# Turning a decode cache's keys: 128x128 transposes on TensorE against 32x32 block turns on VectorE with block transfers, and a changed order of two quads

## The reference

```python
kw = jnp.concatenate([ck_win, k_win], axis=1)          # 512 cached window rows + 4 new
vw = jnp.concatenate([cv_win, v_win], axis=1)
kc = rope(compress(concat(gather_pages(ck_cmp), k_cmp)), cend)
o_cmp, o_sel, o_win = nsa_core(q, pos, kc, vc, cend, overlap, gather_sel, kw, vw, kpos)
```

## Time and profile before

| | |
|---|---|
| median of 3 runs | 589.26 us (589.05 to 589.99) |
| the profiled execution, its own time | 592.85 us |
| its span in the trace | 591.1 us |
| TensorE busy | 560.5 us (95%) |
| VectorE busy | 335.8 us (57%) |
| ScalarE busy | 266.2 us (45%) |
| GpSimd busy | 135.2 us (23%) |

### The profile page before, as it was taken

How to read it: one execution, slowest core, us unless ns; L and a number is a source line. 1 busy time by engine, 2 the same in 40 slices (tenths; PEclk the granted TensorE clock), 3 DMA queues, 4 the chain that set the end, 5 groups by cost and what they waited for, 6 DMA issues and landing times.

```text
span 591.1 us, 12729 instructions
## 1 busy us (share of the span) xinstructions
PE 560.5 (95%) x5102; PEld 505.4 (85%) x5102; DVE 335.8 (57%) x830; ACT 266.2 (45%) x601; POOL 135.2 (23%) x237
## 2 busy tenths in 40 slices
PE   6899999999988999998899999999999999999994
PEld 4899999989977899797689787676778999999994
DVE  5633222488748665336327548858766257773465
ACT  5434435444413352433233267767777253223333
POOL 0016323121101121460330005556453300000000
PEclk9899999999969999999999999999999999999998
DMA  9437722553227234492382215755355533415103
GB/s 300 167 93 220 255 73 71 213 175 128 78 68 243 82 92 123 144 333 95 96 296 72 69 41 142 192 149 143 92 151 134 149 110 108 144 37 176 42 8 145
DMA packets 59468, 80.51 MB, mean 136 GB/s; under 512 B 7249, under 2 KB 48145, under 8 KB 59154
## 3 DMA queue, kind: packets, MB, share of 16 engines
q1 hardware_dynamic: 48320, 49.44, 26.9%
q0 software_dynamic: 10368, 29.14, 15.8%
q10 hardware_dynamic: 722, 1.12, 0.5%
HBM read 65.23 MB, written 8.13 MB: 124 GB/s over the span
## 4 chain that ended last, share of the span: by engine, by line
PE 60%; DVE 5%; ACT 2%; issue 1%; ACTq 0%; DVEq 0%
PE m L1698 40%; PE s L2005 4%; PE o L2012 3%; PE t L1907 1%; PE s L1880 1%; PE s L1881 1%; PE s L1883 1%; PE o L1966 1%; PE t L1844 1%; PE s L1921 1%; PE m L1782 1%; PE o L1992 1%; PE t L1985 1%; DVE w_lo L1272 1%; PE t L1978 1%
## 5 line engine op out<-in xcount | busy, mean ns | idle before, releaser
L1698 PE MATMUL m<-h_hi,w_hi 128*128 128x272 f32 x448 | 134.0, 299 | 0.5 <-DVE w_lo L1272 0.5
L1698 PE MATMUL m<-h_hi,w_lo 128*128 128x272 f32 x448 | 129.2, 288 | 0.0
L1698 PE MATMUL m<-h_lo,w_hi 128*128 128x272 f32 x448 | 128.8, 287 | 0.0
L1698 PE MATMUL m<-w_hi,h_hi 128*128 128x256 f32 (+2 forms) x360 | 105.4, 293 | 2.8 <-issue 1.9
L1698 PE MATMUL m<-w_lo,h_hi 128*128 128x256 f32 (+2 forms) x360 | 102.8, 286 | 0.0
L1698 PE MATMUL m<-w_hi,h_lo 128*128 128x256 f32 (+2 forms) x360 | 102.8, 286 | 0.0
L1272 DVE TENSOR_TENSOR w_lo<-raw,w_hi 128x1024 fp32r<-128x1024 f32 (+2 forms) x62 | 71.1, 1154 | 42.9 <-ACT w_hi L1003 42.9
L1698 PEld LDWEIGHTS m<-h_hi,w_hi 128*128 128x128 f32 x448 | 84.2, 188 | 12.3 <-issue 10.9
L1698 PEld LDWEIGHTS m<-h_lo,w_hi 128*128 128x128 f32 x448 | 84.5, 189 | 0.0
L1698 PEld LDWEIGHTS m<-h_hi,w_lo 128*128 128x128 f32 x448 | 84.5, 189 | 0.0
L955 POOL DMA_DIRECT2D U<-p_turn x108 | 58.1, 546 | 102.7 <-DVE p_turn L1604 94.8
(11 more groups left out here) (296 smaller groups left out, 961.3 us busy)
## 6 DMA issues: line engine op xcount, KB each, us to landing
raw<-in_w_in SPq DMA_DIRECT2D x36, 512.0 KB, 3.8
U<-in_x_p SPq DMA_DIRECT2D x8, 512.0 KB, 5.4
raw<-in_w_o SPq DMA_DIRECT2D x8, 512.0 KB, 3.7
U<-p_turn POOLq DMA_DIRECT2D x54, 64.0 KB, 2.5
U<-p_turn SPq DMA_DIRECT2D x42, 64.0 KB, 2.9
raw<-in_w_in SPq DMA_DIRECT2D x8, 256.0 KB, 3.2
U<-in_ck_win POOLq DMA_DIRECT2D x8, 256.0 KB, 3.2
U<-in_cv_win POOLq DMA_DIRECT2D x8, 256.0 KB, 6.3
```

The source lines that it names most:

```text
L1698: ins = mm(out, lhs(a, k), rhs(b, k), start=(k == 0 and a + b == 0), stop=(k == n - 1 and a == 1))
```

## The change

The keys are no longer turned by TensorE. Step `kt` is now VectorE's alone: two 32x32-block transposes of 128x256 from the key ring into a buffer `key_turn` (two of them). A new step `km` moves the chunk's 16 blocks of 32 partitions x 512 floats (64 KB each) to their places in `keysT` (two buffers): ten from SyncE, six from GpSimd, each behind a wait for the chunk's four turns (`wait_keys_free`). `qkS` waits for the moves. The key ring has four slots, freed by VectorE's turns. GpSimd loads the selected values of the first quad between the turns of chunk 2 (`load_values`) and the others in a new step `v_load`. The order of the stretch is written out anew; it holds the same 19 `main` groups. Scores of the second quad's chunk 0 come ahead of the first quad's `s_exp`, those of chunk 1 after its `s_scale`, those of chunk 2 after its `s_out`.

```diff
@@ -152,10 +152,6 @@
-AFTER_KEYS = (1, 1, 1)
-AFTER_STEP = [(1, 1, 1, 1, 1, 1),
-              (1, 1, 1, 1, 1, 1)]
-
@@ -278,19 +274,48 @@
+
+    def keys(q, c):
+        order.extend(("kt", q, c, b) for b in range(QB))
+
+    keys(0, 0)
+    order += [("km", 0, 0)]
     main(1)
     order += [("mix", u1[3]), ("kc", NCH - 1)]
-    for q in range(NQ):
-        for c in range(3):
-            order += [("kt", q, c, b) for b in range(QB)]
-            main(AFTER_KEYS[c])
-            order += [("qkS", q, c)]
-        for n, step in enumerate(("s_max", "s_turn", "s_imp", "s_mask", "s_exp", "s_scale")):
-            if (q, step) == (NQ - 1, "s_scale"):
-                order += [("cs", 0)]
-            order += [(step, q)]
-            main(AFTER_STEP[q][n])
-        order += [("s_pv", q), ("s_out", q)]
+    main(1)
+    keys(0, 1)
+    order += [("km", 0, 1)]
+    main(1)
+    order += [("qkS", 0, 0)]
+    main(1)
+    keys(0, 2)
+    order += [("km", 0, 2)]
+    main(1)
+    order += [("qkS", 0, 1)]
+    main(2)
+    order += [("qkS", 0, 2), ("s_max", 0), ("v_load", 0)]
+    keys(1, 0)
+    order += [("km", 1, 0)]
+    main(1)
+    order += [("s_turn", 0)]
+    main(1)
+    order += [("s_imp", 0)]
+    keys(1, 1)
+    main(1)
+    order += [("s_mask", 0)]
+    main(1)
+    order += [("qkS", 1, 0), ("km", 1, 1), ("s_exp", 0)]
+    main(1)
+    keys(1, 2)
+    order += [("s_scale", 0)]
+    main(1)
+    order += [("qkS", 1, 1), ("km", 1, 2), ("s_pv", 0), ("s_out", 0), ("qkS", 1, 2), ("v_load", 1)]
+    for step in ("s_max", "s_turn", "s_imp", "s_mask", "s_exp", "s_scale"):
+        if step == "s_scale":
+            order += [("cs", 0)]
+        order += [(step, 1)]
+        main(1)
+    order += [("s_pv", 1), ("s_out", 1)]
@@ -411,8 +436,6 @@
-    if kind == "kt":
-        return ["act" if s[2] == 2 or (s[2] + s[3]) % 2 == 0 else "dve"]
@@ -429,9 +452,11 @@
-KEY_RING = 2 * RING
+KEY_RING = 4
...
+KEYS_AT = (0, 1, 0, 1, 1, 1)
+KEYS_BY_SYNC = 10
@@ -453,7 +478,7 @@
-    return load_turned(len(LOADS) - RING + n // 2) if n < KEY_RING else T_AT[KEYS[n - KEY_RING]] + 1
+    return load_turned(len(LOADS) - RING + n // 2)
@@ -560,7 +585,7 @@
-        key_ring = U[:, 8192:11264].rearrange("p (r c) -> p r c", r=KEY_RING)
+        key_ring = U[:, 8192:10240].rearrange("p (r c) -> p r c", r=KEY_RING)
@@ -574,8 +599,9 @@
-        keysT = U[:, 6144:8192].rearrange("p (b n) -> p b n", b=QB)
-        ptr = [U[:, 7680:8192], U[:, 12928:13440]]
+        keysT = [U[:, 4096:6144], U[:, 6144:8192]]
+        key_turn = [(prm[:, 0:1024], prm[:, 1024:2048]), (placed("key_turn", 3072, [P, 1024])[:, :], U[:, 10240:11264])]
+        ptr = [pm("b_sp"), U[:, 12928:13440]]
@@ -620,6 +646,8 @@
+        key_turned = sem("key_turned")
+        k_moved, k_moved_pool = [sem(f"k_moved{n}") for n in range(2)], [sem(f"k_moved_pool{n}") for n in range(2)]
@@ -668,15 +696,29 @@
+        def key_move(q, c, n):
+
+            f, a = divmod(n, 4)
+            src = key_turn[(3 * q + c) % 2][f // 2][32 * a:32 * a + 32, 512 * (f % 2):512 * (f % 2) + 512]
+            return keysT[KEYS_AT[3 * q + c]][32 * f:32 * f + 32, 512 * a:512 * a + 512], src
+
+        def wait_keys_moved(eng, q, c):
+
+            n = 3 * q + c
+            eng.wait_ge(k_moved[n % 2], 16 * KEYS_BY_SYNC * (n // 2 + 1))
+            eng.wait_ge(k_moved_pool[n % 2], 16 * (16 - KEYS_BY_SYNC) * (n // 2 + 1))
+
...
-            if 3 * q + c:
-                eng.wait_ge(qk_done, 3 * q + c)
+            n = 3 * q + c
+            eng.wait_ge(key_turned, QB * (n + 1))
+            if n == 0:
+                eng.wait_ge(hid_sum, NCH)
+                eng.wait_ge(out_done, 16 * N_OUT)
+            elif n == 1:
+                eng.wait_ge(kc_ready, NCH)
...
-                eng.wait_ge(out_done, 16 * N_OUT)
-                eng.wait_ge(kc_ready, NCH)
-            if q and c == 0:
-                eng.wait_ge(o_done, q)
+                eng.wait_ge(qk_done, max(m for m in range(n) if KEYS_AT[m] == KEYS_AT[n]) + 1)
@@ -806,6 +848,11 @@
+                elif s[0] == "km":
+                    _, q, c = s
+                    wait_keys_free(sp, q, c)
+                    for n in range(KEYS_BY_SYNC):
+                        sp.dma_start(*key_move(q, c, n)).then_inc(k_moved[(3 * q + c) % 2], 16)
@@ -895,7 +942,10 @@
-                pool.wait_ge(t_done, key_freed(n))
+                if n < KEY_RING:
+                    pool.wait_ge(t_done, key_freed(n))
+                else:
+                    pool.wait_ge(key_turned, n - KEY_RING + 1)
@@ -903,6 +953,11 @@
+
+            def load_values(b):
+                n = b % QB
+                pool.indirect_dma_start(U[:, n * 1024:n * 1024 + 1024], None, cv_sel,
+                                        bass.IndirectOffsetOnAxis(rows_sb[:, b:b + 1], 0)).then_inc(v_loaded, 16)
@@ -956,19 +1011,26 @@
-                    if c < 2:
-                        continue
-                    if n == 0:
-                        if q == 0:
+                    if (q, c) == (0, 2):
+                        if n == 0:
...
-                            pool.wait_ge(kc_done, NCH)
-                            pool.wait_ge(kc_ready, NCH)
-                        else:
-                            pool.wait_ge(o_done, q)
-                    b = QB * q + n
-                    pool.indirect_dma_start(U[:, n * 1024:n * 1024 + 1024], None, cv_sel,
-                                            bass.IndirectOffsetOnAxis(rows_sb[:, b:b + 1], 0)).then_inc(v_loaded, 16)
-                    pool.dma_start(U[:, 4096 + n * 512:4608 + n * 512], cv_win[b].rearrange("(m r) c -> m (r c)", r=4)).then_inc(v_loaded, 16)
+                        load_values(n)
+                elif s[0] == "km":
+                    _, q, c = s
+                    wait_keys_free(pool, q, c)
+                    for n in range(KEYS_BY_SYNC, 16):
+                        pool.dma_start(*key_move(q, c, n)).then_inc(k_moved_pool[(3 * q + c) % 2], 16)
+                elif s[0] == "v_load":
+                    q = s[1]
+                    if q == 0:
+                        pool.wait_ge(qk_done, 3)
+                    else:
+                        pool.wait_ge(o_done, 1)
+                        for n in range(QB):
+                            load_values(QB + n)
+                    for n in range(QB):
+                        pool.dma_start(U[:, 4096 + n * 512:4608 + n * 512], cv_win[QB * q + n].rearrange("(m r) c -> m (r c)", r=4))\
+                            .then_inc(v_loaded, 16)
@@ -1129,11 +1191,6 @@
-                elif kind == "kt" and t_uses(s) == ["act"]:
-                    _, q, c, b = s
-                    act.wait_ge(t_done, t + 1)
-                    wait_keys_free(act, q, c)
-                    nc.scalar.copy(keysT[:, b, :], TB[t % 2][:, :]).then_inc(t_act, 1)
@@ -1452,11 +1509,21 @@
-                elif kind == "kt" and t_uses(s) == ["dve"]:
+                elif kind == "kt":
...
-                    dve.wait_ge(t_done, t + 1)
-                    wait_keys_free(dve, q, c)
-                    v.tensor_copy(keysT[:, b, :], TB[t % 2][:, :]).then_inc(t_dve, 1)
+                    ld = KEY_AT[s]
+                    n = 3 * q + c
+                    dve.wait_ge(key_loaded[ld % KEY_RING], 16 * (ld // KEY_RING + 1))
+                    if b == 0:
+                        if n >= 2:
+                            wait_keys_moved(dve, *divmod(n - 2, 3))
+                        elif n == 1:
+                            dve.wait_ge(hid_sum, NCH)
+                    src = key_ring[:, ld % KEY_RING, :].rearrange("p (m h f i) -> p h m f i", m=4, h=2, f=2)
+                    for h in range(2):
+                        dst = key_turn[n % 2][h].rearrange("p (f b m i) -> p b m f i", f=2, b=QB, m=4)[:, b, :, :, :]
+                        ins = v.transpose(dst, src[:, h, :, :, :])
+                    ins.then_inc(key_turned, 1)
@@ -1900,25 +1967,22 @@
-                elif kind == "kt":
-                    ld = KEY_AT[s]
-                    pe.wait_ge(key_loaded[ld % KEY_RING], 16 * (ld // KEY_RING + 1))
-                    for m in range(4):
-                        ins = pe.transpose(tb[:, m * P:(m + 1) * P], key_ring[:, ld % KEY_RING, m * P:(m + 1) * P], ident)
-                    ins.then_inc(t_done, 1)
...
-                    for b in range(QB):
-                        wait_evacuated(pe, T_AT[("kt", q, c, b)])
+                    wait_keys_moved(pe, q, c)
...
-                    elif c == 0:
+                    elif q and c == 0:
+                        pe.wait_ge(s_bias2, q)
+                    elif q and c == 2:
...
+                    kx = keysT[KEYS_AT[3 * q + c]].rearrange("p (a b m i) -> p b a m i", a=4, b=QB, m=4)
...
-                        ins = mm(S[c][32 * b:32 * b + 32, :], q_bd[:, QB * q + b, :], keysT[:, b, :], start=True, stop=True)
+                        out = S[c][32 * b:32 * b + 32, :].rearrange("p (m a i) -> p a m i", m=4, a=4)
```

(1 more changed line is left out.)

## The result

The changed kernel takes 605.4 us (median of 4 runs, 600.95 to 607.75) against 589.25 on the same chip: 1.0263 times the time, 95% interval 1.0198 to 1.0327. It is slower, by 2.0 to 3.3%; I had forecast 588.5, and 592.6 as the upper end. The profiled execution took 606.87 us, its span is 605.1, 14.0 more than before.

What follows compares the result with a forecast made beforehand. TensorE, busy for 95% of the span, and its waits bound the kernel. Gone 17.7 us, come 17.6, plus 0.7 of fewer switches: 0.8 earlier, 589.26 - 0.8 = 588.5 us, range 585.2 to 592.6.

Steps and rivals of the forecast that it cites:

- 15.1 + 0.8 + 1.8 + 0.7: TensorE time gone: key transposes 15.1, a wait for weights 0.8, old clock fall 1.8, fewer transpose/group switches 0.7 us.
- ahead of (0,1): First quad, chunk 1: TensorE there at 249.6, keys moved at 251.4, a wait of 1.8 us.
- ahead of (0,2): First quad, chunk 2: TensorE there at 258.6, keys through full transfer engines at 265.3, a wait of 6.7 us.
- ahead of (1,0), `s_mask`: Second quad, chunk 0: scores wait for `s_mask`, whose banks they overwrite, until 283.1; a wait of 2.2 us.
- ahead of (1,1): Second quad, chunk 1: keys moved at 294.2, TensorE there at 290.4 after only two groups; a wait of 3.8 us.
- around the value products: Second quad, chunk 2: moves covered by the first quad's value products; start 303.9 against 295.2 + 7.2, 1.5 us.
- 8.4 us from turned to moved: Each chunk: SyncE's ten moves, the tenth starting after 9 x 0.65 = 5.85 us and landing 2.6 us later.
- the second rival: First quad, chunk 2: gathers hold back GpSimd's six moves, last landing 7.4 us after issue; 592.4 us, chance 0.18.
- one fall of the clock: After the 6.7 us wait of the first quad's chunk 2, TensorE's clock falls once to half, costing 1.6 us.
- the third rival: TensorE's clock falls at every wait, mostly hidden in later waits; 1.9 us more, 590.4 us, chance 0.15.
- VectorE matters only where it is named above: VectorE gains 17 us of turns and loses 8 copies; costed at nothing outside the walked-through steps.
- The two rivals on the slow side: Gathers holding back GpSimd's moves (592.4 us, chance 0.18) and the clock falling at every wait (590.4 us, chance 0.15).

Runs made afterwards that it cites:

- Run 1: Changed kernel with GpSimd's four gathers of the first quad's selected values issued behind its six moves of the third chunk; 599.49 us, one of four runs at 589.91.
- Runs 2: Changed kernel with matmuls of no use ahead of the waits for moved keys of the first five chunks; 603.62 us, 1.0241 times the kernel before.
- run 9: run 5's kernel with matmuls of no use ahead of the waits for keys of (0,0), (0,2), (1,0), (1,1); 594.28 us, 1.0054 times the kernel before.
- Run 3: Changed kernel without the 96 block moves, scores reading the turned blocks in place (wrong elements); 590.55 us, 1.0017 times the kernel before.
- run 6: Run 3's kernel (no moves, wrong elements) with VectorE's later turns as in run 5; 586.25 us, 0.9935 times the kernel before.
- runs 5: Run 1's kernel with VectorE's turns of (1,1) put behind `s_mask` and of (1,2) behind `s_scale`; 596.29 us, 1.0136 times the kernel before.
- run 8: run 7's kernel with both quads' value gathers issued later on GpSimd, not ahead of key gathers; 586.5 us, 0.9937 times the kernel before.
- run 7: Kernel before, TensorE's transposes issued in pairs one group ahead, third key buffer, (1,0)'s scores between `s_pv` and `s_out`; 598.97 us, 1.0168 times.

## Why the prediction was wrong

What went was put at 15.1 + 0.8 + 1.8 + 0.7 = 18.4, and the balance of the measured sum leaves 18.6: this part was right, as far as a balance can say. What came was put at 17.6 and measured 32.6. By its terms:

| term | forecast | measured |
|---|---|---|
| wait ahead of (0,0) | 0 | 2.0 |
| ahead of (0,1) | 1.8 | 0 |
| ahead of (0,2) | 6.7 | 12.8 |
| ahead of (1,0), `s_mask` | 2.2 | 2.9 |
| ahead of (1,1) | 3.8 | 0 |
| around the value products | 1.5 | 3.1 (`s_scale`) |
| half clock | 1.6 | 10.4 |
| other (a gap of 0.75, modelled ends 0.7) | 0 | 1.4 |

**The step that failed first: "8.4 us from turned to moved".** Its issue part was right (0.7 apart), its landing part was not. I took 2.6 us, from moves of the prompt's attention, where the queues together take 0.47 of the transfer engines' time (419 to 461 us). Here the last move landed 4.0 us after its issue at (0,0) and 7.5 at (0,2); from turned to moved it was 10.5 us at (0,0) (233.88 to 244.39). The rows that should have priced it stood beside it: the earlier trace rows with a share of 0.97 and the earlier trace rows, where a gather in the same stretch takes up to 7.4. I used the 7.4 for the second rival, with a chance of 0.18, and not for the sum; there the full engines moved the landing at (0,2) by 0.7 only, through 5.0 MB at 320 GB/s. Measured were 5.30 MB, and 262 to 264 GB/s. At (0,2) the keys came at 273.1, forecast 265.3: 3.3 us of the 7.8 are GpSimd's moves issued later (265.57 against 262.3, mostly because the turns ended 3.5 late, behind groups that the first wait had delayed), 4.5 are the landing. That GpSimd's six stand behind eight gathers was foreseen. Run 1 shows that the place of the four value gathers, on GpSimd's queue and on the transfer engines together, was worth 8.4 us of that wait.

**The second: one fall of the clock, "1.6".** I counted one and got four, 10.4 us, the largest term of the miss. It was the third rival, at 0.15, and I priced even that at 1.9, on the ground that a fall is hidden in the next wait. It is not, where the next wait ends with VectorE, which is late by the same amount. On this the Trainium skill, "TensorE: Matmul & The Clock Gate", section "HAM oscillation — how this bites in real kernels", was the better guide than my one row: by that rule the clock falls at each of the four waits, and the trace agrees, with 0.50 to 0.57 behind each. Runs 2 and 9 show that the clock can be bought back, but part of the time went into later waits (run 9: ahead of (1,1) from 1.0 to 2.7). So the 10.4 are not what would be gained without them, and what the clock alone costs stays open: in run 9's kernel 2 us by the medians, 5 by the ratios and 0.5 by the two profiled executions. Run 1's one execution at 589.91, with a clock of 0.987, may say that it is more; no trace of it is there.

**The third: "VectorE matters only where it is named above".** The turns are 16 us (six times 2.7) on an engine that works in order, and they put waits for transfers ahead of softmax steps. Run 3 takes all moves away and is no faster than before; run 6 takes the turns from ahead of two softmax steps as well and gains 4 to 5 us more, with 2.9 us still lost at the copy that they then precede. The wait for `s_mask` came out near the forecast (2.9 against 2.2) by luck: `s_mask` ended at 292.5, forecast 283.1. The one for `s_scale` was not seen: I let VectorE do the turns of (1,2) behind its group functions and did not ask who waits for `s_scale`.

The waits forecast for (0,1) and (1,1) did not show since TensorE itself was late by then; in runs 5 and 9, where it is earlier, (1,1) waits 1.0 and 2.7, and in run 9 (0,1) waits 1.4.

The two rivals on the slow side and this third cause are not exclusive: one delay feeds the next. I gave them separate chances and separate prices, and the range ended at the price of one. Both at once, at my prices, would have been 592.4 + 1.9 = 594.3, still short.

## What to carry to other kernels

Price a transfer by the landing times of the stretch into which it goes, at that stretch's DMA share, not by the same transfer elsewhere: 64 KB took 2.4 us in one place and 7.5 in another. Where that share is near 1, add up the bytes and divide by a rate measured with the same mix of transfers. Where TensorE is the bound, work moved to an engine that works in order costs its own time plus every transfer it waits for, in front of everything queued behind; ask for each later step on that engine who waits for it, and ask again after moving the work: in runs 5 and 6 the wait only went from `s_scale` to the next copy. Of the kernels here that compute the right result, the fastest keeps the 15 us of transposes and changes when they and the gathers are issued (run 8, 0.6% faster). The block turns with run 8's places for the gathers, and with the turns of (1,2) behind the copy, were not run, so it is not shown that they must lose.

## What the runs showed of the hardware

*Gaps with nothing to wait for.* In run 7, with a DMA share of 0.96 to 1.00, TensorE stood 3.6 us between small matmuls with no semaphore to wait for; in the two runs without moves 2.2 and 2.4 us in the same place. In run 8, with the same matmuls at the same time and the share falling from 0.98 to 0.48 at 252 us, it did not. A full share is not enough for such gaps, though: in the kernel before the same sixteen matmuls ran with none at a share of 1.01, and in run 9 too (265 to 267 us, 1.01).

```profile
254.00:256.00 2.00, 2.00 (x39) 1.21 (x38) 0.94 (x2) 1.35 (x2) 1.69 (x3) 1.00 1.01 401
...
255.52 0.31 PE L1927 MATMUL o<-k_newT,q_bd 128*32 128x32 f32 x16
```

The profile has queues of kind "instruction", so late instructions are an obvious guess, and the name that the expectations of runs 6 and 8 use. The traces do not bear it out: run 7's last packet on such a queue lies in 248 to 251 us, ahead of the gaps, and runs 3 and 6 show none from 252 to 262. The cause is open. The Trainium skill, "Runtime: NRT & Kernel Launch", section "Instruction fetch mechanics", calls the cost of crossing to the next block of instructions mostly hidden; no run here shows whether these gaps are that cost.

*The clock behind waits.* In the kernel after, waits of 2.0, 12.8, 2.9 and 3.1 us were each followed by a granted clock near 0.5; in run 8 waits of 0.85, 1.19 and 0.98 by 1.00. In run 5 a wait of 2.4 us, with transposes just ahead of it, was followed by value products at full clock (1.00 from 297 to 303 us). The length of one wait alone does not tell.
